# Two transformer blocks on one core: four of eight memory-key chunks moved from the attention into the expert slots, a high part made sooner, one tile's normalised rows later, and the last slots weighed in pairs

## The reference, cut to what matters

```python
def first_block(x, ...):                      # x: [1, 256, 1024] float32
    proj = rms_norm(x, attn_norm) @ w_in      # 3072 columns, six groups of 512
    a_out = rms_norm(moba_attention(...))     # 8 heads of 64, causal
    b_out = rms_norm(diff_attention(...))     # 4 heads, two maps each
    x = x + concat(a_out, b_out) @ w_out
    return x + peer_ffn(rms_norm(x, ffn_norm), peer_query, peer_sub_keys, peer_down, peer_up)

def peer_ffn(x, ...):                         # 8 heads, 16 experts a token and head, of 16384
    q = (x @ w_query).reshape(C, 8, 2, 128)
    sc = einsum('thpd,hpnd->thpn', q, sub_keys)
    top_s, top_i = top_k(sc, 16)              # then the best 16 of the 256 sums
    gates = softmax(best_s)
    act = gelu(einsum('cd,chkd->chk', xc, expert_down[experts]))
    return einsum('chk,chkd->cd', gates * act, expert_up[experts])

def second_block(x, mem, ...):
    x = x + three_branch_mixer(rmsnorm(x))    # convolution, stick-breaking, retention, gates
    k, v = split(rmsnorm(mem, norm_mem_g) @ w_xkv)      # of the memory alone: 256 rows
    x = x + (softmax(q(x) @ k.T) @ v) @ w_xo
    x = x + square(relu(rmsnorm(x) @ w_up)) @ w_down
    return rmsnorm(x, final_g)
```

## Time and profile before

| what | us |
|---|---|
| median of 3 runs (1434.15 to 1437.54) | 1435.48 |
| profiled execution, its own time | 1431.49 |
| its span, first to last instruction | 1429.6 |

### The profile page before, as it was taken

How to read it: one execution, slowest core, us unless ns; L and a number is a source line. 1 busy time by engine, 2 the same in 40 slices (tenths; PEclk the granted TensorE clock), 3 DMA queues, 4 the chain that set the end, 5 groups by cost and what they waited for, 6 DMA issues and landing times.

```text
span 1429.6 us, 17394 instructions
## 1 busy us (share of the span) xinstructions
PE 1235.1 (86%) x5876; PEld 875.2 (61%) x5876; DVE 835.6 (58%) x1518; ACT 605.8 (42%) x1278; POOL 910.6 (64%) x541
## 2 busy tenths in 40 slices
PE   7989887888899766777787878999999989999997
PEld 6668684434454322323333323789999978899886
DVE  6776388777876668776767644613553543278401
ACT  5456344434433432323233222447465345555432
POOL 6974485556666447444444441695868854799985
PEclk9999898999999998999989999999999999999999
DMA  7543459999999999999999995464645643456652
GB/s 262 160 137 99 148 186 410 419 419 419 419 419 420 421 419 419 420 421 419 420 420 421 420 419 242 144 199 127 191 130 174 226 129 112 144 186 188 194 186 102
DMA packets 72943, 400.69 MB, mean 280 GB/s; under 512 B 8096, under 2 KB 8352, under 8 KB 39712
## 3 DMA queue, kind: packets, MB, share of 16 engines
q0 software_dynamic: 36864, 268.45, 45.3%
q1 hardware_dynamic: 33696, 123.35, 26.8%
q10 hardware_dynamic: 2304, 7.85, 1.5%
HBM read 396.48 MB, written 3.15 MB: 280 GB/s over the span
## 4 chain that ended last, share of the span: by engine, by line
PE 32%; DMA 22%; POOL 17%; issue 16%; DVE 8%; ACT 3%; another core or an unknown queue 0%; POOLq 0%; ACTq 0%; DVEq 0%
DMA arena<-in_experts,arena 17%; POOL w_lo L1270 14%; PE bank L790 11%; PE bank L557 7%; PE bank L558 6%; PE bank L559 6%; DMA late_rows<-in_experts,arena 5%; DVE arena L1602 2%; POOL arena L1322 2%; POOL stat L1244 1%; DVE late_rows L1602 1%; ACT arena L1100 1%; ACT diag L1106 1%; ACT hT_hi L962 0%
## 5 line engine op out<-in xcount | busy, mean ns | idle before, releaser
L1270 POOL TENSOR_TENSOR w_lo<-ring,w_hi 128x1024 fp32r<-128x1024 f32 x222 | 570.7, 2592 | 160.6 <-ACT w_hi L940 160.0
L790 PE MATMUL bank<-arena,diag 128*128 128x512 f32 x928 | 447.9, 635 | 130.8 <-ACT diag L1106 129.0
L1322 POOL DMA_INDIRECT arena<-in_experts,arena x232 | 267.1, 1151 | 262.8 <-PE bank L790 195.6
L790 PEld LDWEIGHTS bank<-arena,diag 128*128 128x128 f32 x928 | 182.1, 203 | 381.2 <-issue 220.7
L1602 DVE CUSTOM_DVE_ANT_0 arena<-arena 128x1024 f32<-128x1024 f32 x232 | 305.9, 1329 | 165.1 <-DMA arena<-in_experts,arena 163.7
L940 ACT ACTIVATE w_hi<-ring 128x1024 fp32r<-128x1024 f32 x228 | 240.1, 1058 | 184.5 <-PE bank L559 154.4
L557 PE MATMUL bank<-hT_hi,w_hi 128*128 128x256 f32 x736 | 209.4, 285 | 4.2 <-DVE hT_lo L1357 2.7
L558 PE MATMUL bank<-hT_lo,w_hi 128*128 128x256 f32 x736 | 208.2, 283 | 0.0
L559 PE MATMUL bank<-hT_hi,w_lo 128*128 128x256 f32 x736 | 208.2, 283 | 0.0
L1097 ACT ACTIVATE arena<-arena 128x2 f32<-128x2 f32 (+2 forms) x94 | 19.2, 204 | 423.9 <-DVE arena L1602 418.6
L557 PEld LDWEIGHTS bank<-hT_hi,w_hi 128*128 128x128 f32 x736 | 141.2, 192 | 5.3 <-issue 5.1
(11 more groups left out here) (231 smaller groups left out, 1716.5 us busy)
## 6 DMA issues: line engine op xcount, KB each, us to landing
ring<-in_stream SPq DMA_DIRECT2D x228, 512.0 KB
arena<-in_experts,arena POOLq DMA_INDIRECT x232
kv_park<-arena ACTq DMA_DIRECT2D x8, 256.0 KB
arena<-kv_park ACTq DMA_DIRECT2D x1, 2048.0 KB, 9.2
x_res<-in_x SPq DMA_DIRECT2D x2, 512.0 KB, 5.2
arena<-in_mem SPq DMA_DIRECT2D x1, 1024.0 KB, 11.3
arena<-in_sub_keys ACTq DMA_DIRECT2D x1, 1024.0 KB, 5.9
out<-arena SPq DMA_DIRECT2D x2, 512.0 KB, 2.6
```

The lines of the kernel that those rows point to most:

```text
L790: mm = pe.matmul(y_banks[half][:, :], diag[:, slot % DIAGS, :], rows_buf[BUFFER[slot]][:, D + 512 * half:D + 512 * half + 512], start=(i = ...
L1270: nc.gpsimd.tensor_tensor(w_lo[:, slot, :], ring[:, slot, :], w_hi[:, slot, :].bitcast(F32), ALU.subtract).then_inc(S("lo_made"), 1)
L1322: nc.gpsimd.indirect_dma_start(out=rows_buf[b], out_offset=None, in_=experts, in_offset=bass.IndirectOffsetOnAxis(ap=expert_u[:, slot:slot ...
```

## The change

Four of the eight `xk` chunks become `xk_late` and are done among the slots, at the slots 96, 100, 104 and 108, behind `xv`. In the attention two pairs are left, ahead of the steps 3 and 8. The buffers 11 and 12 are used from slot 119 on, not 108; pairs of slots are weighed up to 120, not 112, and again from 240 to 253. ACT calls `hi_parts(LAST["w_out"])` ahead of the squares of the second norm, and makes two high parts of the query chunks ahead of the second square. The rows `xn` of token tile 1 are made at slot 48 instead of ahead of the selection.

```diff
-CHUNK_AT += [CHUNK_AT[-1] + 9 + 4 * i for i in range(8)]
+CHUNK_AT += [CHUNK_AT[-1] + 9 + 4 * i for i in range(12)]
...
-FEW, MORE, PAIRS = 72, 108, 112
+FEW, MORE, PAIRS = 72, 119, 120
...
-BATCHES = [(slot, 2) for slot in range(0, PAIRS, 2)] + [(slot, BATCH) for slot in range(PAIRS, SLOTS - 4, BATCH)]
-BATCHES += [(SLOTS - 4, 2), (SLOTS - 2, 1), (SLOTS - 1, 1)]
+BATCHES = [(slot, 2) for slot in range(0, PAIRS, 2)] + [(slot, BATCH) for slot in range(PAIRS, SLOTS - 16, BATCH)]
+BATCHES += [(slot, 2) for slot in range(SLOTS - 16, SLOTS - 2, 2)] + [(SLOTS - 2, 1), (SLOTS - 1, 1)]
...
-STREAM = [("w_in", 24), ("xk", 8), ("w_out", 8), ("query", 16), ("xv0", 4), ("xv1", 4),
+STREAM = [("w_in", 24), ("xk", 4), ("w_out", 8), ("query", 16), ("xv0", 4), ("xv1", 4), ("xk_late", 4),
...
-MEMORY_STEPS = {("xk", 0): 2, ("xk", 1): 5, ("xk", 2): 8, ("xk", 3): 11}
+MEMORY_STEPS = {("xk", 0): 3, ("xk", 1): 8}
...
+                        if h >= PEER_H + 4:
+                            n = h - PEER_H - 4
+                            if j == 0:
+                                xk_bank = open_bank(pe, ("xk_late", n))
+                            wait_weight(FIRST["xk_late"] + 2 * n + j)
+                            transposed_into(xk_bank[:, j * T:(j + 1) * T], FIRST["xk_late"] + 2 * n + j, None, h_)
...
-                    hi_parts(last - 1 if n == 0 and name != "mix" else last if t == 0 else last + RING - 1)
+                    hi_parts(last + 2 if name == "ffn" and n and not t else last - 1 if n == 0 and name != "mix" else last if t == 0 else last + RING - 1)
...
-            act.wait_ge(S("kv_parked"), 16 * 4)
+            act.wait_ge(S("kv_parked"), 16 * 2)
             act.dma_start(subk, sub_keys).then_inc(S("subk_loaded"), 16)
             act.dma_start(gain_rows, ffn_rows).then_inc(S("gain_loaded"), 16)
+            hi_parts(LAST["w_out"])
             sumsq("ffn", xs, xn, (0,))
...
+                    if slot - 3 in CHUNK_AT[-3::2]:
+                        n = CHUNK_AT[-3::2].index(slot - 3)
+                        act.wait_ge(S("kv_parked"), 16 * (6 + n))
+                        park([(("xk_late", n), None)], "xk_late", n)
                     if slot == CHUNK_AT[-1] + 3:
-                        act.wait_ge(S("kv_parked"), 16 * 6)
-                        park(values(1), "xv", 1)
-                        hi_parts(LAST["xv1"] + RING)
+                        hi_parts(LAST["xk_late"] + RING)
...
-            for t in range(TT):
+
+            def normed_rows(t):
...
+            normed_rows(0)
...
+                    if slot == 3 * PEER_K:
+                        normed_rows(1)
```

More of the change, by code:

```diff
@@ L105 @@
 LAST = {_name: FIRST[_name] + _n - 1 for _name, _n in STREAM}
-BEFORE = {"ffn": "w_out", "mix": "xv1", "xa": "w_o", "mlp": "xo", "final": "mlp_down"}
+BEFORE = {"ffn": "w_out", "mix": "xk_late", "xa": "w_o", "mlp": "xo", "final": "mlp_down"}
 HALVES = {"mix": [(0, 0), (1, 0), (0, 1), (1, 1)]}
@@ L176, in plan @@
             add(key, chunk)
+    for n in range(2):
+        add(("xk_late", n), FIRST["xk_late"] + 2 * n + 1)
     for t in range(TT):
@@ L229, in plan @@
         else:
-            bank = turn % (4 if key[0] in ("query", "sub", "xv") else 8)
+            bank = turn % (4 if key[0] in ("query", "sub", "xv", "xk_late") else 8)
             turn = bank + 1
@@ L380, in build @@
         mem, memn = tiles(A(22784, 2048)), tiles(A(24832, 2048))
-        stage = [A(8192 + 512 * i, 512) for i in range(4)] + [A(7168 + 512 * i, 512) for i in range(2)]
+        stage = [A(8192 + 512 * i, 512) for i in range(2)] + [A(7168 + 512 * i, 512) for i in range(2)]
         hd_ss = [stats(16) for _ in range(4)]
@@ L772, in _ @@
                     slot = t * n_tile + i
-                    if slot in (CHUNK_AT[-8], CHUNK_AT[-4]):
-                        xv_banks = [open_bank(pe, ("xv", int(slot == CHUNK_AT[-4]), tile)) for tile in range(TT)]
+                    if slot in (CHUNK_AT[-12], CHUNK_AT[-8]):
+                        xv_banks = [open_bank(pe, ("xv", int(slot == CHUNK_AT[-8]), tile)) for tile in range(TT)]
                     if slot in CHUNK_AT:
@@ L1036, in park @@
                 for i, (key, _) in enumerate(keys):
-                    piece = n if name == "xk" else 4 + 2 * i + n
-                    place = stage[n if name == "xk" else 4 + i]
+                    piece = n if name == "xk" else 2 + n if name == "xk_late" else 4 + 2 * i + n
+                    place = stage[2 + n if name == "xk_late" else n if name == "xk" else 2 + i]
                     copy_out(key, place)
@@ L1132, in _ @@
                         sub_out(SUB_AT[slot - 2])
+                    if slot == CHUNK_AT[-9] + 3:
+                        park(values(0), "xv", 0)
                     if slot == CHUNK_AT[-5] + 3:
-                        park(values(0), "xv", 0)
+                        act.wait_ge(S("kv_parked"), 16 * 4)
+                        park(values(1), "xv", 1)
+                    if slot - 3 in CHUNK_AT[-3::2]:
+                        n = CHUNK_AT[-3::2].index(slot - 3)
+                        act.wait_ge(S("kv_parked"), 16 * (6 + n))
+                        park([(("xk_late", n), None)], "xk_late", n)
                     if slot == CHUNK_AT[-1] + 3:
-                        act.wait_ge(S("kv_parked"), 16 * 6)
-                        park(values(1), "xv", 1)
-                        hi_parts(LAST["xv1"] + RING)
+                        hi_parts(LAST["xk_late"] + RING)
                     if k == 15 and u + 2 < UNITS:
@@ L1318, in gather @@
                 elif b >= 11:
-                    pool.wait_ge(chunk_done, LAST["xv1"] + 1)
+                    pool.wait_ge(chunk_done, LAST["xk_late"] + 1)
                 elif b >= 8:
@@ L1329, in _ @@
                     lo_parts(FIRST["query"] + 2 * AHEAD_HEADS + LOW_AT[slot])
-                if slot == CHUNK_AT[-4] + 3 * PEER_K:
-                    lo_parts(LAST["xv1"] + RING)
+                if slot == CHUNK_AT[-1] + 2 * PEER_K:
+                    lo_parts(LAST["xk_late"] + RING)
                 if slot == (PEER_H + 2) * PEER_K:
@@ L1619, in _ @@
             dve.wait_ge(S("gain_loaded"), 16)
[L1620 removed]
+            def normed_rows(t):
                 dve.wait_ge(S("rstd"), 2 * seq["ffn"] + t + 1)
[L1622 removed]
+                own.link(v.scalar_tensor_tensor(xn[:, t, :], xs[:, t, :], rstd["ffn"][:, t:t + 1], gain_rows,
                                                 ALU.mult, ALU.mult))
[L1624 removed]
+            normed_rows(0)
             for u in range(2):
```

7 lines of the change are left out of this document (3 added, 4 removed).

## The result

Before 1434.15 us, after 1425.11 us (medians of five runs each: 1431.52 to 1437.54 and 1420.18 to 1426.38). The ratio is 0.9926, with an interval of 0.9911 to 0.9942: by it the kernel takes 10.6 us less, between 8.3 and 12.8, while the two medians lie 9.0 apart. The forecast was 1423.3. The profiled execution after took 1424.0 us with a span of 1422.2, against 1431.49 and 1429.6.

A forecast was written before the change was run, and what follows sets the result against it. Ahead of the slots PE's order and waits bound the kernel, in the slots the bytes, at their end PE's leftover work. From the 1435.48 us median, -10 - 6.4 + 6.2 - 2 gave 1423.3 us, range 1415 to 1431.

The forecast's parts named there:

- The sum: Whole kernel: 10 and 6.4 us saved, 6.2 added, 2 saved, so 12.2 us off the median, giving 1423.3.
- Two pairs fewer: Attention: removing two pairs, 11.7 us of PE, brings DVE's turn to the last heads 10 us earlier; bounds 4.7 to 13.9.
- costs DVE about 2.5 us of waiting: Attention: the second pair, ahead of step 8, runs from about 116 to 122 and makes DVE wait that long.
- The locks: Attention: DVE instructions held up by POOL's low parts lost 4.2 and about 2.2 us; only one such low part stays.
- The high part: End of `w_out`: made ahead of the square, it ends PE's stall and starts the transposes 6.4 us sooner; bounds 3.5 to 7.
- Rows later: Ahead of the selection: moving tile 1's rows to slot 48 saves 0 to 1 us and costs nothing there.
- The end in pairs: End of the slots: PE finishes 2 us sooner behind the last diagonal matrix; not over 2.9.
- The slots: Slot stage: four chunks and two parks, 2.62 MB, add 6.2 us of transfers; 5.0 to 9.
- the stage would end only 4 us longer: Sign in the profile after: the slot stage up to PE's last slot grows 4 us, 6.2 less 2.
- The attention gives half: Rival, attention: DVE becomes the bound, only the last pair's wait goes, 5 us, giving 1428; chance 0.13.
- The slower one: Rival, end of slots: pairs keep PE at half clock for the last 16 slots, giving 1440; chance 0.08.
- The low end of the range, 1415: Larger gain, with slots at 5.0, the `w_out` term at 7 and the end at 2.9.

The follow-up runs named there:

- e3: Changed kernel with the high part of the last `w_out` chunk back behind the first square, and the later one back too; ratio to before 0.9958.
- e7: Changed kernel with the last sixteen slots in fours again, then two, one, one; PE's tail 4.66 us against 2.40.
- e9: Changed kernel with its second `xk` pair behind the turns of the differential heads, not ahead of step 8; ratio to before 0.9935.
- e11: Changed kernel making only the first of three products per matmul in the four early `xk` chunks; attention 36.41 us against 38.86.
- e8: Kernel before, profiled a second time with nothing edited; slots 681.74 us against 679.59.
- e1: Kernel before plus the earlier high part, later rows and end in pairs, all four pairs staying in the attention; ratio to before 0.9929.
- e12: Changed kernel with one `xk` pair among the slots, two ahead of steps 3 and 8, one behind the differential heads' turns; ratio to before 0.9931.
- e2: Changed kernel making only the first of three products per matmul in the four late `xk` chunks; ratio to before 0.992, slots 687.04 us.
- e6: Changed kernel with the rows of tile 1 back ahead of the selection, not at slot 48; ratio to before 0.9935.

## Why the prediction held, and where its terms were off

**The sum.** Predicted -10 - 6.4 + 6.2 - 2 = -12.2. Measured by stages, with means where several runs show one: -7.9 (attention), -5.8 (w_out), -1.1 (selection, most of it by the high part too), +6.9 (slots: 688.1 less 681.2), -2.3 (tail) = -10.2, against the 10.6 that the ratio gives. The -7.9 is that of the executions with the higher clock; with the same instructions e3 and e7 gained 6.4 and 6.7 there. The total came out nearer than its terms: 2.1 and 0.6 us too much at the attention and the high part stand against 1.1 at the selection that the sum did not have, and that part is luck. The first gather came 14.6 us sooner, at 191.47, not 16.4. For the move of the chunks alone the forecast had -10 + 6.2 = -3.8; it is worth about -1. The single pair of profiles gives only -7.4, since its slots hold the short 679.6 of before.

**Two pairs fewer: mis-sized, 7.9 for 10.** The step that failed is "costs DVE about 2.5 us of waiting" for the second pair; it cost 4.85 in after and 6.1 in e7. I let that pair run from 116 to 122. It started at 116.89, since PE itself had waited 1.31 and 1.73 us for DVE ahead of it, and took 6.7 us, 0.85 over full speed. The turns and values ahead of it took 1.76 us (115.13 to 116.89), where the same instructions at full clock took 1.10 (109.36 to 110.46). So about 1.5 of the 2.35 us too few are the clock, and the rest was a lead of PE over DVE that wasn't there. That is what the step left out: I costed every matmul at the full clock of before. With 11.7 us of work gone PE waits for DVE in the attention, and the granted clock falls: 0.72 from 114 to 120 us in after, behind the waits of 1.31 and 1.73, 0.50 over the same 6 us in e7, and 0.50 for 12 us where still more is taken away (e9, e11). In e7 the wait behind the pair is 1.2 us longer than in after, and so is the attention.

A low clock at the start of the attention is another matter. Over its first 4 us it was 0.69 in e8, where nothing is changed, 0.59 in e1 and 0.60 in e3 and e12. With the old order it costs nothing (46.78 and 46.86 beside 46.76); with the new one it costs 1.5 us (40.3 beside 38.9), since DVE now waits 2.32 for the first pair and not 0.80. So the change doesn't cause this one, but no longer hides it. That the clock and not an edit makes these differences rests on executions whose instructions in the attention are the same (after, e2, e3, e6, e7); the clock itself was not varied alone.

The Trainium skill, "TensorE: Matmul & The Clock Gate", section "HAM oscillation — how this bites in real kernels", says that waits between bursts throw the engine back to half rate. I weighed it at the end of the slots, where it did not bite (1.00); the trace agrees with it in the attention (0.72 behind the two waits), where I had not asked.

**The locks.** L1504 was to take 2.5 to 3 us at 100.8 and took 0.75: a low part less beside it, and the other a moment later. I took 10 because it lay close to the 9.2 of waits, but DVE's waits over the stage fell only by 1.4 us; the other 6.5 are busy time, 6.4 of it the two locked pairs of instructions (4.97 to 0.75, 2.71 to 0.55). That alone doesn't make the locks the cause. e12 has one lock of 2.2 us more than e3, at the same clock, and waits 2.2 less for PE behind it (e12, then e3):

```profile
120.89 2.71 DVE L1519 TENSOR_SCALAR arena<-arena,stat 128x128 f32<-128x128 f32 x2
...
126.99 0.42 DVE L1545 COPY arena<-bank 128x256 f32<-128x256 f32 x1 [2.61 <-PE bank L681]
```

```profile
126.92 0.42 DVE L1539 COPY arena<-bank 128x256 f32<-128x256 f32 x1 [4.77 <-PE bank L678]
```

Their attention took 40.33 and 40.32 us: that lock lay in time in which DVE would have waited anyway. How the 7.9 us divide between PE's work and the locks was not tried apart. e9 shows a lock elsewhere. Its scaling of the differential heads, 128x1024 with two SBUF inputs, took 1.22 us between two low parts of POOL, where after's took 2.67 under one:

```profile
138.47 1.22 DVE L1534 TENSOR_TENSOR arena<-arena,stat 128x1024 f32<-128x1024 f32 x1
```

**The high part: right, 5.8 for 6.4,** and by e3 0.95 on top in the selection, of which I had taken nothing into the sum. With 6.7 us it is the largest net gain of the change. The transposes came at 167.13; 164.2 was the sum of two terms, of which the attention's was 2.1 too large and this one 0.6.

**Rows later: right,** 0.25 us. **The end in pairs: right,** 2.3 for 2, and the clock stayed up.

**The slots: right in kind, 6.9 for 6.2,** inside its bounds of 5 to 9, and bytes: two thirds of the matmuls taken away gave back 1.7 at most, and the stage's mean rate is 411 GB/s with and without the late chunks. Over slots 96 to 120 the transfers stayed at 1.01 as predicted. That the stage would end only 4 us longer read wrong in the pair of profiles (+6.8 up to PE's end), by the dips at its start.

**The rivals.** "The attention gives half" was the nearest of them in mechanism, though its 5 us lie farther from 7.9 than my 10. The slower one, by the clock at the end, did not come. The low end of the range, 1415, does not follow from its terms: 1423.3 - 4 - 1.2 - 0.6 - 0.9 is 1416.6. What no rival said is e1's result: the move of the chunks nets about 1 us, and all of the rest comes from the smaller parts.

## What to carry to other kernels

Work moved from a stage bound by order to one bound by bytes pays its bytes in full, and gives back less than its own time: here 11.7 us of TensorE's work gave 7.9 and cost 6.9. Take the small edits of a change apart before crediting the large one; one high part made a few instructions sooner gave 6.7 us. And where TensorE loses work but not its waits, cost what is left at the clock that it will then be granted, not at that of before.

## What was not expected of the hardware

Less work on TensorE made the same stretch barely faster twice: 38.9 to 38.3 us with a pair of 5.85 taken out (e9), 38.9 to 36.4 with 7.8 us (e11), at a granted clock of 0.50 for 12 us at a stretch (1.2 GHz), with the engine shown as busy throughout. And the start of the attention, ahead of any edit, lay between 96.3 and 100.2 us in fourteen profiles: marks relative to it repeat to 0.1 us where the clock stands the same, absolute times don't.
